# Sums of halves of the normalised input on GpSimd or VectorE, ahead of three seven-product stages

## The chip, the cores and the metric

One core of a Trainium2 chip runs the whole program. The time is the device time of one execution in microseconds (us). The engines named are TensorE (PE in the profile), VectorE (DVE), ScalarE (ACT), GpSimd (POOL), and SyncE (SP), which issues most of the loads of weights.

## The reference

Two blocks of a network on a sequence of 512 positions of 1024 features, in float32. The first block puts 16 learned positions in front (528 in all) and has two layers. Each layer is a mixer, a layer norm, a multilayer perceptron with squared ReLU, and a layer norm:

```python
h = _layer_norm(DEEPNORM_ALPHA * h + mix, ln_g[layer, 0], ln_b[layer, 0])
h = _layer_norm(DEEPNORM_ALPHA * h + _sq_relu_mlp(h, ffn_w1[layer], ffn_w2[layer]),
                ln_g[layer, 1], ln_b[layer, 1])
```

with `_sq_relu_mlp(h, w1, w2) = square(relu(h @ w1)) @ w2`. The mixer of layer 0 is an attention, that of layer 1 a retention, which begins with `proj = h @ w_in`. The second block (sparse attention beside a state-space scan, then a gated feed-forward part) comes behind them. The change touches only the first matrix product behind three of the layer norms: the perceptron's `h @ w1` of layer 0 (behind the norm ln00) and of layer 1 (behind ln10), and the retention's `h @ w_in` (behind ln01).

## The kernel before, in words

**Layout and arithmetic.** The activations lie in `x32`, features on the 128 partitions: 8 tiles (KT) of 528 columns, a column for each position. Every matrix product is made of three fast ones: each operand is split into a high part and a rest (`x_hi`, `x_lo`; `w_hi`, `w_lo`), and TensorE adds hi x hi, hi x lo and lo x hi. ScalarE makes the high parts (`split_hi`, L362, for weights), VectorE the rests (`split_lo`, L370). Weights come in chunks of 128 x 1024 into a ring of four (`raw`), and each engine's program splits three chunks ahead (AHEAD) of the chunk that TensorE multiplies.

**The norm and the first tiles.** At the end of a layer norm VectorE scales tile after tile (L1404), ScalarE writes the normalised tile to `x32` (L1434, counted by the semaphore `norm_y`) and its high part to `x_hi` (L1437), and VectorE the rest to `x_lo` (L1410, counted by `norm_lo`). TensorE starts while this goes on: `first_two` multiplies two chunks at the same time, tile by tile, and before each of the eight tiles it waits for that tile's `x_lo`. The last tile is number 7.

**Seven products.** A product of a 2 x 2 grid of blocks is made of seven block products instead of eight, for which sums of halves of both operands are needed. Sums of halves of the weights are made in memory by DMAs that GpSimd issues (`SUM_PARTS`, L327 to L349). Sums of halves of the input are made by `turn_sum` (L1461 to L1471), four of them, each of 128 x 1056 elements (128 x 1024 in layer 1's perceptron): 

```python
(t1, x[:, 0:4, first], x[:, 0:4, second], ALU.subtract),
(t2, t1, x[:, 4:8, second], ALU.add),
(self.fourth(), t2, x[:, 4:8, first], ALU.subtract),
(t3, x[:, 4:8, second], x[:, 0:4, second], ALU.subtract)
```

Sum 1 waits for all eight tiles (`norm_y`), sums 2 and 3 for the one before each (`turns_made`). `turn_hi` (ScalarE, L1477) and `turn_lo` (VectorE, L1486 and L1488) split them, number 0 to 3 in the order in which TensorE reads them. TensorE's `seven_pe` (L1546) waits for `turns_lo` at the first block of the kinds 5, 6, 7 and 4.

**Order of the work around the change.** Each engine has one queue in program order, written out by hand. Behind ln00 and ln10 stands the stage "up" (`up0a`, `up1a`): four chunks in the ordinary way, two of them in `first_two`. Behind it comes `seven0a` or `seven1a`. `Mlp.act` and `Mlp.dve` say what ScalarE and VectorE do during "up": ScalarE evicts each tile (`positive`, L1702), VectorE squares it (`square`, L1742), ScalarE takes the high part (`high`, L1706), VectorE the rest (`low`, L1746), with `split(0)` to `split(3)` and the turns between. Each `positive(t)` for t of 2 or more waits for `square(t - 2)`, since the buffers are two. `last_parts` puts turn_lo of 2 and 3 into the first blocks of the seven-product stage. Behind ln01 stands `ret0`, four chunks, then `sevenr0`; `retention_act` and `retention_dve` give the order there.

In the seven-product stage ScalarE copies block products out of PSUM (L1609) and VectorE adds the next ones to the copies (L1647); TensorE waits for a copy before it goes on in the same bank.

**GpSimd's queue** is `even_loads`, `ret_loads`, `dsa_loads`. `ret_loads` issues the copies and sums of the weights of later stages, each behind a wait for a chunk that TensorE has done, and the load of `decay` for each retention head, the first of them behind the last `x_lo` of ln01 (L1824). GpSimd does no arithmetic in the first block but a few memsets. In the second block it adds `select` and `bias_near` (L2307), 64 times, beside VectorE's work of the sparse attention.

Of the kernel before, what the change touches and what calls it, by code (L numbers as in the profile page):

```python
# [7 lines left out]
ALU = mybir.AluOpType  # L8
# [6 lines left out]
KT = D // P  # L15
# [187 lines left out]
def program(nc, x_in, weights, params, tables, lam_in, w_uk, w_uv, rel, line, skewed, cum_dram, acum_dram, merged_dram, kept_dram, gate_dram, sums_dram, out):  # L203
    with ExitStack() as ctx:
# [10 lines left out]
        x32 = sb("x32", [P, KT, T])  # L215
# [257 lines left out]
        for p, (kind, h, j) in enumerate(products):  # L473
            n = sum(len(m) for m in maps.values())
# [676 lines left out]
        def only_split(eng, split, name):  # L1151
# [8 lines left out]
        norm_squared, norm_var, norm_root, norm_scaled, norm_y, norm_hi, norm_lo = (  # L1160
            sem(f"norm_{n}") for n in ("squared", "var", "root", "scaled", "y", "hi", "lo"))
        mlp_squared, hidden_hi, hidden_lo = sem("mlp_squared"), sem("hidden_hi"), sem("hidden_lo")
        seven_done, seven_summed, seven_kept = (sem(f"seven_{n}") for n in ("done", "summed", "kept"))
        turns_made, turns_hi, turns_lo = (sem(f"turns_{n}") for n in ("made", "hi", "lo"))
# [274 lines left out]
        class Halves:  # L1439
# [13 lines left out]

                return self.fourth_rows.rearrange("p a (k n) -> p (a k) n", k=2)[:, :, 0:self.w]

            def source(self, dve, norm):

                dve.wait_ge(norm_y, KT * (norm.nl + 1))
                return x32

            def turn_sum(self, dve, norm, n):  # L1461
                first, second, w = self.cols(0), self.cols(1), self.w
# [92 lines left out]
        class Mlp(Halves):  # L1555
# [138 lines left out]
            def act(self, act, next_norm):  # L1694
                name = f"up{self.layer}a"

                def positive(t):
                    u = FIRST_TILE[name] + t
                    act.wait_ge(chunk_done, FIRST_CHUNK[name] + t + 1)
                    wait(act, mlp_squared, 32 * self.layer + t - 1)  # L1700
                    src = early_out(t, self.wide) if t < 2 else tile_out(Step(u), self.wide)
                    nc.scalar.activation(halves(self.pos[:, t % 2], self.wide), src, ACT.Relu).then_inc(evicted[u % 2], 1)  # L1702

                def high(t):
                    act.wait_ge(mlp_squared, 32 * self.layer + t + 1)
                    nc.scalar.activation(halves(self.h_hi[:, t], self.wide), halves(self.sq[:, t % 2], self.wide), ACT.Copy).then_inc(hidden_hi, 1)  # L1706

                def split(t):
                    split_hi(act, Step(FIRST_CHUNK[name] + t + AHEAD))
                split(0)  # L1710
                self.turn_hi(act, 0)
                self.turn_hi(act, 1)
                positive(0)
                positive(1)
                split(1)
                high(0)
                high(1)
                positive(2)
                split(2)
                self.turn_hi(act, 2)  # L1720
                positive(3)
                high(2)
                split(3)
                high(3)
                self.turn_hi(act, 3)
                for half, hn in enumerate("ab"):
                    self.seven_act(act, f"seven{self.layer}{hn}")
                    if half:
                        before_norm_act(act, f"down{self.layer}{hn}", next_norm)
                    else:  # L1730
                        only_split(act, split_hi, f"down{self.layer}{hn}")

            def dve(self, dve, norm, next_norm):
                name = f"up{self.layer}a"

                def square(t):
                    u = FIRST_TILE[name] + t
                    dve.wait_ge(evicted[u % 2], u // 2 + 1)
                    if t >= 2:
                        dve.wait_ge(hidden_lo, 32 * self.layer + t - 1)  # L1740
                    pos, sq = halves(self.pos[:, t % 2], self.wide), halves(self.sq[:, t % 2], self.wide)
                    nc.vector.tensor_tensor(sq, pos, pos, ALU.mult).then_inc(mlp_squared, 1)  # L1742

                def low(t):
                    dve.wait_ge(hidden_hi, 32 * self.layer + t + 1)
                    nc.vector.tensor_tensor(halves(self.h_lo[:, t], self.wide), halves(self.sq[:, t % 2], self.wide),  # L1746
                                            halves(self.h_hi[:, t], self.wide), ALU.subtract).then_inc(hidden_lo, 1)

                def split(t):
                    split_lo(dve, Step(FIRST_CHUNK[name] + t + AHEAD))  # L1750
                self.turn_sum(dve, norm, 0)
                self.turn_sum(dve, norm, 1)
                split(0)
                self.turn_lo(dve, 0)
                square(0)
                square(1)
                split(1)
                low(0)
                low(1)
                self.turn_sum(dve, norm, 2)  # L1760
                self.turn_sum(dve, norm, 3)
                square(2)
                self.turn_lo(dve, 1)
                split(2)
                square(3)
                low(2)
                split(3)

                def last_parts():
                    self.turn_lo(dve, 2)  # L1770
                    low(3)
                    self.turn_lo(dve, 3)
                for half, hn in enumerate("ab"):
                    self.seven_dve(dve, f"seven{self.layer}{hn}", None if half else last_parts)
                    if half:
                        before_norm_dve(dve, f"down{self.layer}{hn}", 1.0, next_norm)
                    else:
                        residual_dve(dve, f"down{self.layer}{hn}", self.wide, ALPHA)

        ln00 = LayerNorm("ln00", FIRST_TILE["up0a"], True, PARAM["ln_g"], PARAM["ln_b"])  # L1780
        mlp0 = Mlp(0, True)
# [28 lines left out]
        def ret_loads(pool):  # L1810

            for part in SUM_PARTS:
                part(pool, 2)
            for h, name in ((2, "down0a"), (3, "down0b")):
                pool.wait_ge(chunk_done, FIRST_CHUNK[name])
                for part in SUM_PARTS:
                    part(pool, 1 + h)
            for h in range(RET_HEADS):
                if h == 0:
                    pool.wait_ge(norm_lo, ln01.lo_at)  # L1820
                else:
                    pool.wait_ge(ret_decayed, 5 * h)
                a = TABLE["decay"] + h * DECAYS
                pool.dma_start(decay[:], tables[:, a:a + DECAYS]).then_inc(decay_in, 16)  # L1824
                pool.wait_ge(chunk_done, FIRST_CHUNK[("sevenr1", "ro0", "ro1", "ret_out1")[h]])
                for part in ((sums_copy,), (sums_of_two,), (sums_of_three, sums_of_four), ())[h]:
                    part(pool, 5)
            for name, parts in (("ret_out1", SUM_PARTS[:2]), ("down1a", SUM_PARTS[2:])):
                pool.wait_ge(chunk_done, FIRST_CHUNK[name])
                for part in parts:  # L1830
                    part(pool, 6)
            pool.wait_ge(chunk_done, FIRST_CHUNK["down1b"])
            for part in SUM_PARTS:
                part(pool, FFN_SUMS)
            sums_copy(pool, FFN_SUMS + 1)

        class Retention(Halves):
# [14 lines left out]
            def part(self, h, i, row, half):  # L1852

                kind, n = self.pairs(h)[i]
                skip = META if kind in "qg" and half == 0 else 0
                start = half * HALF - (META if kind in "qg" and half else 0)
                buf = {"q": rq, "k": rk, "v": v_raw, "g": rg}[kind]
                return buf[:, 2 * n + row, start:start + HALF - skip], slice(skip, HALF)
# [78 lines left out]
        ret = Retention()  # L1937
# [238 lines left out]

        def retention_dve(dve):
            for c in range(4):
                if c < 2:
                    ret.turn_sum(dve, ln01, 2 * c)  # L2180
                    ret.turn_sum(dve, ln01, 2 * c + 1)
                split_lo(dve, Step(FIRST_CHUNK["ret0"] + c + AHEAD))
                if c < 3:
                    ret.turn_lo(dve, c)
            ret.turn_lo(dve, 3)
            for h in range(RET_HEADS):
                ret.dve(dve, h)
                if h in (1, 2):
                    for ck in range(4):
                        split_lo(dve, Step(FIRST_CHUNK[f"ro{h - 1}"] + ck + AHEAD))  # L2190
                        ret_residual_dve(dve, h - 1, ck, ALPHA if h == 1 else 1.0)
                ret_keys_dve(dve, h)
            split_lo(dve, Step(FIRST_CHUNK["ret_out1"] + AHEAD))
            for n in range(8):
                ret_gate_dve(dve, LAST_HEAD, n)
            for e in range(4):
                ret_lo_dve(dve, LAST_HEAD, e)
            before_norm_dve(dve, "ret_out1", 1.0, ln10, outs=[open_out(t) for t in range(OPEN)], split_before=1)
# [1578 lines left out]
```

## Time and profile before

| | us |
|---|---|
| median of 3 runs | 2663.25 |
| lowest and highest | 2659.4, 2663.29 |
| span of the profiled execution, first to last instruction | 2656.4 |
| TensorE busy | 2615.0 (98%) |
| VectorE busy | 1675.5 (63%) |
| ScalarE busy | 1268.0 (48%) |
| GpSimd busy | 183.4 (7%) |

The profile is of one execution; what lies around its span (3.0 to 6.9 us against the three runs) isn't in the trace, and its own time is not given beside the page. Starts are in us from the start of the span. A row of a timeline has the start, the length, the engine, the line of the kernel, the operation, what it writes and reads, the shape, how many instructions are merged in the row, and in brackets how long the engine stood idle before it and who released it. In the chain that ended last TensorE has 85% of the span, VectorE 8%, ScalarE 4%. TensorE's granted clock was 1.00 in all stretches around the change.

### The profile page before, as it was taken

Reading aid. Unit: us, or ns where it says so; the run is one execution under the profiler, and the core shown is the slowest. Engines: PE = TensorE matmul, PEld = TensorE weight load, DVE = VectorE, ACT = ScalarE, POOL = GpSimd, SP = SyncE. Lnnn points to the kernel's source line nnn. Section 1 sums busy time; section 2 is a strip of 40 time slices with the busy share of each in tenths; the row PEclk is TensorE's granted clock in tenths of the full one; section 3 lists DMA queues with packets and bytes.
Section 4 is the critical chain, followed back from the end, with each engine's and each line's share of the span. In section 5 each row is a group of like instructions: output and inputs, shape, how many; then the busy total and the mean of one; then the engine's idle time right before and its main releaser. Section 6 shows DMA issues by size and latency. Waiting matters only on the chain.

```text
span 2656.4 us, 42476 instructions
## 1 busy us (share of the span) xinstructions
PE 2615.0 (98%) x16497; PEld 2236.1 (84%) x16497; DVE 1675.5 (63%) x2902; ACT 1268.0 (48%) x2049; POOL 183.4 (7%) x234
## 2 busy tenths in 40 slices
PE   9999999999999999999999999999999999999998
PEld 9877799999999798779898786766877777799996
DVE  4544586264565465487265535875589987696784
ACT  4556365153454354365154434254365564475561
POOL 1111000000000000100000012051000000000000
PEclk9999999999999999999999999999999999999999
DMA  9994936858556564736557979922433333254451
GB/s 355 222 230 119 216 92 234 207 165 248 135 171 212 146 184 140 232 110 196 145 164 245 260 187 266 253 66 80 145 94 114 119 111 120 81 189 148 156 174 56
DMA packets 187722, 450.56 MB, mean 170 GB/s; under 512 B 14984, under 2 KB 31368, under 8 KB 186896
## 3 DMA queue, kind: packets, MB, share of 16 engines
q1 hardware_dynamic: 108368, 264.29, 29.4%
q0 software_dynamic: 60000, 167.78, 26.7%
q10 hardware_dynamic: 19168, 15.93, 2.0%
q8 instruction: 127, 2.08, 0.3%
q14 instruction: 59, 0.48, 0.1%
HBM read 438.24 MB, written 159.51 MB: 225 GB/s over the span
## 4 chain that ended last, share of the span: by engine, by line
PE 85%; DVE 8%; ACT 4%; issue 2%; DMA 0%; POOL 0%; DVEq 0%; ACTq 0%; POOLq 0%
PE ps L399 29%; PE ps L1546 25%; PE ps L549 6%; PE ps L3344 4%; PE ps L2354 2%; PE ps L1991 2%; PE ps L2145 2%; PE ps L2029 2%; PE ps L2891 2%; PE ps L791 2%; PE ps L919 2%; DVE w_lo L370 1%; PE ps L878 1%; ACT w_hi L362 1%; DVE xs L3044 1%
## 5 line engine op out<-in xcount | busy, mean ns | idle before, releaser
L370 DVE TENSOR_TENSOR w_lo<-raw,w_hi 128x1024 fp32r<-128x1024 f32 x500 | 611.1, 1223 | 467.1 <-ACT w_hi L362 466.1
L362 ACT ACTIVATE w_hi<-raw 128x1024 fp32r<-128x1024 f32 x500 | 527.1, 1055 | 512.9 <-PE ps L399 292.3
L1546 PE MATMUL ps<-x_hi,w_hi 128*128 128x264 f32 (+1 forms) x1120 | 317.4, 283 | 2.1 <-DVE rg L1925 0.7
L1546 PE MATMUL ps<-x_hi,w_lo 128*128 128x264 f32 (+1 forms) x1120 | 316.3, 282 | 0.0
L1546 PE MATMUL ps<-x_lo,w_hi 128*128 128x264 f32 (+1 forms) x1120 | 316.1, 282 | 0.0
L399 PE MATMUL ps<-x_hi,w_hi 128*128 128x512 f32 (+1 forms) x688 | 248.3, 378 | 4.4 <-DVE x_lo L1410 2.7
L399 PE MATMUL ps<-x_lo,w_hi 128*128 128x512 f32 (+1 forms) x688 | 244.3, 372 | 0.0
L399 PE MATMUL ps<-x_hi,w_lo 128*128 128x512 f32 (+1 forms) x688 | 243.2, 371 | 0.0
L1546 PEld LDWEIGHTS ps<-x_hi,w_hi 128*128 128x128 f32 x1120 | 210.8, 188 | 5.0 <-issue 2.2
L1546 PEld LDWEIGHTS ps<-x_hi,w_lo 128*128 128x128 f32 x1120 | 211.1, 188 | 0.0
L1546 PEld LDWEIGHTS ps<-x_lo,w_hi 128*128 128x128 f32 x1120 | 210.6, 188 | 0.4
L399 PE MATMUL ps<-h_hi,w_hi 128*128 128x264 f32 (+1 forms) x768 | 205.7, 322 | 0.0
L399 PE MATMUL ps<-h_lo,w_hi 128*128 128x264 f32 (+1 forms) x768 | 205.1, 322 | 0.0
L399 PE MATMUL ps<-h_hi,w_lo 128*128 128x264 f32 (+1 forms) x768 | 204.6, 320 | 0.0
L399 PEld LDWEIGHTS ps<-x_hi,w_hi 128*128 128x128 f32 x688 | 124.6, 188 | 39.3 <-issue 16.4
L399 PEld LDWEIGHTS ps<-x_hi,w_lo 128*128 128x128 f32 x688 | 124.6, 188 | 23.3
L399 PEld LDWEIGHTS ps<-x_lo,w_hi 128*128 128x128 f32 x688 | 124.5, 188 | 22.8 <-issue 1.0
L399 PEld LDWEIGHTS ps<-h_lo,w_hi 128*128 128x128 f32 x768 | 127.7, 188 | 11.6 <-issue 0.2
L399 PEld LDWEIGHTS ps<-h_hi,w_lo 128*128 128x128 f32 x768 | 127.8, 189 | 11.2
L399 PEld LDWEIGHTS ps<-h_hi,w_hi 128*128 128x128 f32 x768 | 127.1, 188 | 11.6 <-issue 0.2
L549 PE MATMUL ps<-x_hi,w_hi 128*128 128x264 f32 x352 | 111.9, 318 | 0.0
L549 PE MATMUL ps<-x_lo,w_hi 128*128 128x264 f32 x352 | 99.9, 284 | 0.0
(503 smaller groups left out, 5827.8 us busy)
## 6 DMA issues: line engine op xcount, KB each, us to landing
raw<-in_weights SPq DMA_DIRECT2D x255, 512.0 KB
raw<-weight_sums SPq DMA_DIRECT2D x280, 256.0 KB
weight_sums<-in_weights POOLq DMA_DIRECT2D x36, 1536.0 KB, 19.4
raw<-in_weights SPq DMA_DIRECT2D x210, 256.0 KB
weight_sums<-in_weights POOLq DMA_DIRECT2D x12, 2048.0 KB, 31.1
weight_sums<-in_weights POOLq DMA_DIRECT2D x12, 1792.0 KB, 22.1
weight_sums<-weight_sums POOLq DMA_DIRECT2D x12, 1536.0 KB, 14.3
weight_sums<-weight_sums POOLq DMA_DIRECT2D x4, 2048.0 KB, 19.7
```

Source lines behind the costliest of these rows:

```text
L362: nc.scalar.activation(w_hi[:, s], raw[:, s], ACT.Copy).then_inc(hi_ready, 1)
L370: nc.vector.tensor_tensor(w_lo[:, s], raw[:, s], w_hi[:, s], ALU.subtract).then_inc(lo_ready, 1)
L399: last = nc.tensor.matmul(o[:, h, :], w[:, s, k], a[:, k0 + k, cols], start=start and k == 0 and n == 0, stop=stop and k == nk - 1 and n == 2)
L549: last = nc.tensor.matmul(ps[:, 2 + h, 0:HALF], a[:, g % RING, w], b[:, k, cols], start=k == 0 and n == 0, stop=half_end and n == 2)
L791: last = nc.tensor.matmul(flat[0:n, o + a:o + b], qk[rows, qt, c:c + n], qk[rows, kt_, a:b], start=True, stop=True)
L919: last = nc.tensor.matmul(flat[rows, 3072 + (first - 1) * P:3072 + SEQ], vt[0:k, group_of(p) % 2, b, col:col + wide], turned_from(p, b, fi ...
L1546: last = nc.tensor.matmul(out_, w[:, s, 4 * (b % 2) + k], a, start=kind in "125" and k == n == 0, stop=k == 3 and n == 2, skip_group_check ...
L1991: last = nc.tensor.matmul(flat[:, o + SEQ - w:o + SEQ], rv[0:n, b, e * P:(e + 1) * P], decayed[0:n, b, SEQ - w:SEQ], start=b == 0, stop=b ...
L2029: last = nc.tensor.matmul(ps[:, 2 * (u % 2), 0:SEQ], w[:, g % RING, 2 * f + m], a[:, f], start=f == 0 and n == 0, stop=f == 3 and n == 2)
L2145: last = nc.tensor.matmul(open_out(t)[:, 0, :], w[:, g % RING, k], a[:, k % 4], start=k == 0 and n == 0, stop=k == KT - 1 and n == 2)
L2354: last = nc.tensor.matmul(kept_out_at(n)[:, 0, :], w[:, ck % RING, k], a[:, k, META:T], start=k == 0 and i == 0, stop=k == KT - 1 and i == 2)
L3344: last = nc.tensor.matmul(out_, w[:, g % RING, n], a[:, r], start=n == 0 and m == 0, stop=n == len(rows) - 1 and m == 2)
```

## The change

`turn_sum_pool` does with GpSimd what `turn_sum` does with VectorE, and is called for the three stages from `ret_loads`. The twelve calls of `turn_sum` go from VectorE's queue. On ScalarE `positive(0)` moves ahead of `turn_hi(1)`, and on VectorE `square(0)` ahead of `turn_lo(0)`. The stage ahead of `sevenf` in the second block keeps `turn_sum` on VectorE.

```diff
+            def turn_sum_pool(self, pool, norm, n):
+                first, second, w = self.cols(0), self.cols(1), self.w
+                t1, t2, t3 = (self.t_raw[:, m, :, 0:w] for m in range(3))
+                if n == 0:
+                    pool.wait_ge(norm_y, KT * (norm.nl + 1))
+                if n in (1, 2):
+                    pool.wait_ge(turns_made, 4 * self.turn + n)
+                out_, a, b, op = ((t1, x32[:, 0:4, first], x32[:, 0:4, second], ALU.subtract),
+                                  (t2, t1, x32[:, 4:8, second], ALU.add),
+                                  (self.fourth(), t2, x32[:, 4:8, first], ALU.subtract),
+                                  (t3, x32[:, 4:8, second], x32[:, 0:4, second], ALU.subtract))[n]
+                nc.gpsimd.tensor_tensor(out_, a, b, op).then_inc(turns_made, 1)
...
                 split(0)
                 self.turn_hi(act, 0)
+                positive(0)
                 self.turn_hi(act, 1)
-                positive(0)
                 positive(1)
...
-                self.turn_sum(dve, norm, 0)
-                self.turn_sum(dve, norm, 1)
                 split(0)
+                square(0)
                 self.turn_lo(dve, 0)
-                square(0)
                 square(1)
                 split(1)
                 low(0)
                 low(1)
-                self.turn_sum(dve, norm, 2)
-                self.turn_sum(dve, norm, 3)
                 square(2)
...
             for part in SUM_PARTS:
                 part(pool, 2)
+            for n in range(4):
+                mlp0.turn_sum_pool(pool, ln00, n)
             for h, name in ((2, "down0a"), (3, "down0b")):
...
                 if h == 0:
+                    for n in range(4):
+                        ret.turn_sum_pool(pool, ln01, n)
                     pool.wait_ge(norm_lo, ln01.lo_at)
...
                     part(pool, 6)
+                if name == "ret_out1":
+                    for n in range(4):
+                        mlp1.turn_sum_pool(pool, ln10, n)
             pool.wait_ge(chunk_done, FIRST_CHUNK["down1b"])
...
         def retention_dve(dve):
             for c in range(4):
-                if c < 2:
-                    ret.turn_sum(dve, ln01, 2 * c)
-                    ret.turn_sum(dve, ln01, 2 * c + 1)
                 split_lo(dve, Step(FIRST_CHUNK["ret0"] + c + AHEAD))
```

## Rows read from the trace of the kernel before

**Rows 1.** The page: its first line, and busy time, share and count of TensorE.

```profile
span 2656.4 us, 42476 instructions
...
PE 2615.0 (98%) x16497; PEld 2236.1 (84%) x16497; DVE 1675.5 (63%) x2902; ACT 1268.0 (48%) x2049; POOL 183.4 (7%) x234
```

**Rows 2.** Timeline of TensorE in seven0a and seven1a (start, length, instruction, [idle before]).

```profile
385.25 0.39 PE L1546 MATMUL ps<-t_hi,w_hi 128*128 128x264 f32 x1 [0.55 <-ACT h_u L1609]
...
394.55 0.40 PE L1546 MATMUL ps<-x_hi,w_hi 128*128 128x264 f32 x1 [0.25 <-DVE h_z L1647]
...
1195.48 0.39 PE L1546 MATMUL ps<-t_hi,w_hi 128*128 128x256 f32 x1 [0.58 <-ACT h_u L1609]
...
1204.66 0.38 PE L1546 MATMUL ps<-x_hi,w_hi 128*128 128x256 f32 x1 [0.39 <-DVE h_z L1647]
```

**Rows 3.** GpSimd's groups by form (busy, mean ns), and one addition in its timeline.

```profile
L2307 POOL TENSOR_TENSOR combo<-select,bias_near 128x256 f32<-128x256 f32 x48 | 35.2, 757 | 31.1 <-DVE d_stat L2585 31.1
...
L2307 POOL TENSOR_TENSOR combo<-select,bias_near 128x128 f32<-128x128 f32 x16 | 7.0, 459 | 6.1 <-DVE d_stat L2585 6.0
...
1732.84 0.72 POOL L2307 TENSOR_TENSOR combo<-select,bias_near 128x256 f32<-128x256 f32 x1
```

**Rows 4.** Timelines of VectorE and GpSimd where an addition met VectorE's work.

```profile
1730.38 1.22 DVE L370 TENSOR_TENSOR w_lo<-raw,w_hi 128x1024 fp32r<-128x1024 f32 x1 [1.51 <-ACT w_hi L362]
...
1730.48 1.71 POOL L2307 TENSOR_TENSOR combo<-select,bias_near 128x256 f32<-128x256 f32 x1
...
1738.10 2.26 DVE L2601 TENSOR_SCALAR d_buf<-d_buf,d_stat 128x384 f32<-128x384 f32 x1
...
1739.42 0.71 POOL L2307 TENSOR_TENSOR combo<-select,bias_near 128x256 f32<-128x256 f32 x1
...
1740.28 0.41 DVE L2601 TENSOR_SCALAR d_buf<-d_buf,d_stat 128x384 f32<-128x384 f32 x1
```

**Rows 5.** Timelines of ScalarE, VectorE and TensorE from ln00 into the stage up0a.

```profile
364.48 0.83 ACT L1434 ACTIVATE x<-ln_xc,par 128x528 f32<-128x528 f32 x1
...
366.02 0.71 DVE L1410 TENSOR_TENSOR x_lo<-x,x_hi 128x528 fp32r<-128x528 f32 x1 [0.79 <-ACT x_hi L1437]
...
366.65 1.25 DVE L1471 TENSOR_TENSOR t_raw<-x 128x1056 f32<-128x1056 f32 x1
...
367.00 0.40 PE L399 MATMUL ps<-x_hi,w_hi 128*128 128x264 f32 x2
...
369.55 1.22 DVE L370 TENSOR_TENSOR w_lo<-raw,w_hi 128x1024 fp32r<-128x1024 f32 x1
...
381.02 0.71 DVE L1742 TENSOR_TENSOR h_sq<-h_pos 128x528 f32<-128x528 f32 x1 [0.21 <-ACT h_pos L1702]
...
382.37 0.63 ACT L1706 ACTIVATE h_hi<-h_sq 128x528 fp32r<-128x528 f32 x1
```

**Rows 6.** The same from ln01 into ret0 and the first block of sevenr0.

```profile
732.27 0.83 ACT L1434 ACTIVATE x<-ln_xc,par 128x528 f32<-128x528 f32 x1
...
734.67 0.47 PE L399 MATMUL ps<-x_hi,w_hi 128*128 128x512 f32 x1
...
747.86 0.29 PE L1546 MATMUL ps<-x_hi,w_hi 128*128 128x264 f32 x1
```

**Rows 7.** Timeline of ScalarE from ln10 into the stage up1a.

```profile
1175.54 0.82 ACT L1434 ACTIVATE x<-ln_xc,par 128x512 f32<-128x512 f32 x1
...
1192.64 0.62 ACT L1706 ACTIVATE h_hi<-h_sq 128x512 fp32r<-128x512 f32 x1
```

**Rows 8.** Timelines of GpSimd around the three places, and of VectorE at decay's first reader.

```profile
443.47 1.68 POOL L327 DMA_DIRECT2D weight_sums<-in_weights  x2 [118.57 <-PE ps L1546]
...
734.82 0.60 POOL L1824 DMA_DIRECT2D decay<-in_tables  x1 [45.90 <-DVE x_lo L1410]
...
791.07 0.69 DVE L2077 SCALAR_TENSOR_TENSOR decayed<-ps,decay 128x512 f32<-128x512 f32 x1 [1.36 <-PE ps L1968]
...
1252.46 1.50 POOL L344 DMA_DIRECT2D weight_sums<-weight_sums  x1 [134.29 <-PE ps L1546]
```

More of the change, by code:

```diff
@@ L1454, in fourth @@
                 return self.fourth_rows.rearrange("p a (k n) -> p (a k) n", k=2)[:, :, 0:self.w]
-            def source(self, dve, norm):
-                dve.wait_ge(norm_y, KT * (norm.nl + 1))
-                return x32
+            def turn_sum_pool(self, pool, norm, n):
[10 more added lines that the diff above has]
+                nc.gpsimd.tensor_tensor(out_, a, b, op).then_inc(turns_made, 1)
             def turn_sum(self, dve, norm, n):
```

## Prediction, on record before the changed kernel had run

> **What bounds the kernel now.** I read the page first. TensorE is busy 98% of the span [rows 1], so a part that moves off VectorE pays only where TensorE stands still for VectorE. The next view is TensorE's timeline from the end of each of the three layer norms (the last tile of the normalised input is there at 365.3, 733.1 and 1176.4 us) to the first dozen blocks of the seven-product stage. In stage seven0a there are two pauses, 0.55 us behind ScalarE's copy L1609 and 0.25 us behind VectorE's sum L1647; in seven1a the same two, 0.58 and 0.39 us; in the retention stage there is none [rows 2]. The reader should see that all the idle time in reach is 0.55 + 0.25 + 0.58 + 0.39 = 1.77 us, 0.07% of the span. Such a change can't be a clear gain; the question is what it can cost.
>
> **What is removed.** Twelve VectorE instructions, four a stage, of 1.25 us in the record. From one start to the next it is 0.08 us less (the last x_lo has 0.71 us, and the sum behind it starts 0.63 us later), so 1.17 us each and 4.7 us a stage [rows 5]. Two stand ahead of the first weight split, right behind the last x_lo, two in the middle of the stage "up". What hid them is TensorE's work on the four tiles of "up" (or of ret0), and that cover stays.
>
> **What is added: twelve GpSimd instructions.** The trace before has no GpSimd addition of this size. The nearest rows are L2307's: 757 ns for 256 columns and 459 ns for 128 in the mean, 0.72 us for one of 256 that nothing disturbed [rows 3]. The slope is (757 - 459)/128 = 2.33 ns a column. From the mean, 1056 columns take 0.757 + 800 x 0.00233 = 2.62 us. The mean holds some disturbed ones; with the undisturbed 0.72 less the 0.459 of 128 the slope is 2.04 ns, and the time 0.72 + 800 x 0.00204 = 2.35 us. I take 2.5 us, between two near ends; four make 10 us, twice what VectorE took. Alone they would do no harm: in the first stage sum 1 would be ready at 367.9, sum 2 near 370.7 and the last by 376.
>
> **Whether the two engines can work at the same time** decides. Near 1730 us VectorE began a weight split w_lo (two inputs in SBUF) 0.10 us ahead of a GpSimd addition. The split took its usual 1.22 us; the addition took 1.71 us instead of 0.72, so it waited for the whole of the split [rows 4]. The other order is there for another VectorE form: a TENSOR_SCALAR that met additions under way took 2.26 us against 0.41 us for its twin just after, so it got free at 1738.10 + 2.26 - 0.41 = 1739.95, 0.2 us before the last record of the GpSimd run ended at 1740.13 [rows 4]. No row shows a two-input VectorE instruction meeting an addition in the middle. Its cost lies between nothing (it goes on, as that w_lo did over the last 0.13 us of the GpSimd record before it) and the rest of the addition, 2.5 - 0.2 = 2.3 us. I take 2.3 us: the split and the addition shut each other out in the one case where they met, and the reverse is seen with a VectorE instruction that asks for less data. Its own ends are 2.35 - 0.2 = 2.15 us and the full 2.62 us.
>
> The Trainium skill (SBUF — State Buffer, section "Who interferes with whom") says that a VectorE instruction with two SBUF inputs contends with a GpSimd instruction that reads SBUF, and that the second to issue is blocked until the first is done. By it the sum below stands; if it held for no two-input instruction the sum would be about -0.6 us. The trace agrees for one order, with the 1.71 us; the other is not shown for this form.
>
> **Stage seven0a, step by step.** GpSimd waits for norm_y. ScalarE's last tile ends at 364.48 + 0.83 = 365.31, so sum 1 starts at about 365.4. The last x_lo (L1410) is issued at 366.02, since it waits for one more ScalarE instruction [rows 5]. So sum 1 is always first, by 0.6 us. In the old order the sums were queued behind this x_lo; now it stands behind a sum. It goes at 365.4 + 2.3 = 367.7 and ends at 368.4 instead of 366.73. TensorE's last column of the first two tiles began at 367.00 [rows 5] and needs it; with 0.15 us from release to start it begins at 368.55: 1.55 us lost at once.
>
> Then both queues are full. The three other sums and VectorE's work take turns, and VectorE has no idle time in which to hide them. Up to square(3) it has three w_lo (1.22 - 0.08 = 1.14 us from start to start), two turn_lo (of the sums' size, 1.17), four squares and two h_lo (of x_lo's size, 0.62) [rows 5]: 3.4 + 2.3 + 3.7 = 9.5 us rounded. Starting 0.6 us after 367.7, square(3) is done at 368.3 + 9.5 + 3 x 2.3 = 384.7. Before it ended at 381.73, and h_hi of that tile started at 382.37, because ScalarE's own queue was not there sooner [rows 5]. Now h_hi waits for VectorE and starts at 384.8, 2.4 us late. Behind it on ScalarE stand turn_hi(3), a w_hi and the copy L1609 for which TensorE was already waiting at 385.25 [rows 2]. So that block comes at 387.7: 2.4 us in all for the stage, the 1.55 included, not beside it.
>
> **Stage seven1a**: the last tile ends at 1176.36 [rows 7], sums of 1024 columns take 0.1 us less, so x_lo gets free at 1178.65; 0.6 + 9.3 + 3 x 2.2 = 16.5 us later, 1195.15, square(3) is done, and h_hi starts at 1195.2 instead of 1192.64 [rows 7]: 2.6 us.
>
> **Retention stage**: x_lo goes at 733.10 + 0.1 + 2.3 = 735.5, TensorE at 736.35 instead of 734.67 [rows 6]: 1.7 us. There are no squares and no h_lo here. VectorE reaches the w_lo that the first of the seven products needs after x_lo, one w_lo, a turn_lo and the three later sums, at about 736.1 + 1.1 + 1.2 + 3 x 2.3 = 745.3, so it is done at 746.5; TensorE asked for it at 747.86 before and asks at 749.6 now [rows 6]. Nothing more is lost.
>
> **Edits at nothing.** GpSimd's queue: it stood idle for 118.6 us before 443.47 and for 134.3 us before 1252.46, so nothing is late behind the sums of the first and third stage; behind those of the second is the load of decay, moved from 734.82 to near 745. Its first reader is at 791.07 [rows 8], which leaves 45 us. No other queue is passed. positive(0) ahead of turn_hi(1) on ScalarE costs nothing while square(0) is hidden; turn_hi(1) comes a microsecond later, and positive(1) with it, ahead of squares that VectorE reaches later still. The third user, the stage before sevenf, keeps its sums on VectorE.
>
> **The sum** is 2.4 + 1.7 + 2.6 = 6.7 us. With 2.15 us for each hold it is 5.4 (four holds on the path in two stages, one in the third), with 2.62 us 9.6. The profiled execution has a span of 2656.4 us [rows 1]; the three runs lie 3.0 to 6.9 us above it, for what stands around the span and for scatter. Its own time isn't given, so I add the sum to the median: 2663.25 + 6.7 = 2670.0 us.
>
> **Rivals.**
> - No hold in the order that matters: VectorE's two-input work goes on beside GpSimd. For it speaks that w_lo over the end of a GpSimd record; against it the addition that waited 1.0 us. VectorE then is free 4.7 us earlier and the pauses that it ends itself, 0.25 + 0.39 = 0.64 us, go; ScalarE's copies after TensorE's own work keep theirs. 2662.6 us, 2661.5 if all four went: not slower. It decides if the last x_lo keeps its 0.7 us in all stages.
> - Held only once a stage: after x_lo VectorE's queue keeps GpSimd out until VectorE waits for a sum itself, in time that it has gained. 1.55 + 1.7 + about 1.55 = 4.8 us, 2668.0 us. For it speaks that VectorE was first in the one clean meeting.
> - The additions run much slower than the slope says (rows of 264 with a stride, three reads in each stage from x): at twice 2.5 us each hold is 2.5 us longer, four on the path in two stages and one in the third, 6.7 + 9 x 2.5 = 29 us, 2692 us. Nothing in the trace asks for it.
>
> **How the numbers follow.** Forecast 0.60, no hold 0.26, held once 0.09, far slower sums 0.05. A measurement of this kernel can tell about 0.2%, 5.3 us, from no change. The forecast's own range is 5.4 to 9.6 us, and with the scatter of the runs (3.9 us among three) a fifth of it may still fall inside 5.3: slower 0.60 x 0.82 + 0.05 + 0.02 = 0.56; same 0.11 + 0.22 + 0.07 = 0.40; faster 0.04, from the rival without holds and a low set of runs. The range of 8 in 10 goes from 2661.0, which takes in most of that rival, to 2675.0, above the forecast's upper end of 2672.9 with scatter; alone, the forecast's range is 2667.5 to 2674.
>
> **What would show it.** Right: in each stage the last x_lo in the record lasts about 2.4 us, or starts that late, and TensorE pauses 1.5 us before the eighth column of "up"; the first GpSimd sum takes 2.5 us, the next ones more; VectorE's w_lo and turn_lo there show 2 to 3.5 us; the wait of seven0a behind L1609 grows from 0.55 to some 1.4 us. Wrong: x_lo at 0.7 us with a GpSimd sum running beside it, or TensorE's gaps at the same places and lengths as before.

## The result, and the profile after

The changed kernel takes 2666.82 us (median of 20 runs, 2664.39 to 2673.91) against 2659.36 us (20 runs beside it, 2658.09 to 2664.36): ratio 1.0026, 95% interval 1.0019 to 1.0032. That is 6.9 us slower by the ratio (5.1 to 8.5) and 7.5 us by the two medians, where 6.7 was forecast. In absolute terms the forecast of 2670.0 is 3.2 us high, because it stood on a median of three runs (2663.25) that was itself 3.9 us above that of the twenty.

The page of the changed kernel, the lines that answer to [rows 1]:

```profile
span 2663.2 us, 42470 instructions
...
PE 2615.6 (98%) x16497; PEld 2236.1 (84%) x16497; DVE 1685.9 (63%) x2890; ACT 1268.2 (48%) x2049; POOL 218.3 (8%) x246
```

The span is 6.8 us longer, TensorE's busy time is the same within 0.6 us: TensorE waits more. VectorE is busy 10.4 us more with twelve instructions fewer, so others of its instructions last longer. GpSimd's four sums of the first stage, in its timeline:

```profile
365.50 2.45 POOL L1467 TENSOR_TENSOR t_raw<-x 128x1056 f32<-128x1056 f32 x1 [36.65 <-ACT x L1434]
...
368.04 2.81 POOL L1467 TENSOR_TENSOR t_raw<-t_raw,x 128x1056 f32<-128x1056 f32 x1
...
370.93 3.34 POOL L1467 TENSOR_TENSOR h_raw<-t_raw,x 128x1056 f32<-128x1056 f32 x1
...
374.21 2.94 POOL L1467 TENSOR_TENSOR t_raw<-x 128x1056 f32<-128x1056 f32 x1
```

The first took 2.45 us, from the moment when the tile was there; the others 2.81 to 3.34 us. The excess is time in which VectorE's instruction was still at work: x_lo ended at 368.52, 0.48 us behind the start of sum 2, and 2.81 less 0.48 is 2.33. The next view is the timeline of VectorE, and its last row that of ScalarE, in the same stretch; they answer to [rows 5]:

```profile
366.13 2.39 DVE L1410 TENSOR_TENSOR x_lo<-x,x_hi 128x528 fp32r<-128x528 f32 x1 [0.80 <-ACT x_hi L1437]
...
368.44 3.48 DVE L370 TENSOR_TENSOR w_lo<-raw,w_hi 128x1024 fp32r<-128x1024 f32 x1
...
371.86 2.98 DVE L1750 TENSOR_TENSOR h_sq<-h_pos 128x528 f32<-128x528 f32 x1
...
374.76 3.52 DVE L1496 TENSOR_TENSOR t_lo<-t_raw,t_hi 128x1056 fp32r<-128x1056 f32 x1
...
384.12 0.69 DVE L1750 TENSOR_TENSOR h_sq<-h_pos 128x528 f32<-128x528 f32 x1
...
384.84 0.65 ACT L1714 ACTIVATE h_hi<-h_sq 128x528 fp32r<-128x528 f32 x1 [0.62 <-DVE h_sq L1750]
```

Each of the first four VectorE rows has its usual length plus a hold: x_lo 2.39 us instead of 0.71, w_lo 3.48 instead of 1.22, a square 2.98 instead of 0.70, turn_lo 3.52 instead of 1.25. The two queues take turns: if each hold ends one usual length before its row does, x_lo got free at 367.81, 0.14 us before sum 1's record ended, then sum 2 when x_lo was done, w_lo when sum 2 nearly was, and so on. Four VectorE rows a stage are held in this way, and the twelve holds, less the twelve sums that VectorE no longer makes, are its 10.4 us. Square(3) ended at 384.81 instead of 381.73, and h_hi waited for it. All pauses of TensorE in the three stages, which answer to [rows 2], [rows 6] and [rows 7]:

```profile
368.67 0.36 PE L399 MATMUL ps<-x_hi,w_hi 128*128 128x264 f32 x1 [1.40 <-DVE x_lo L1410]
...
387.74 0.39 PE L1554 MATMUL ps<-t_hi,w_hi 128*128 128x264 f32 x1 [1.28 <-ACT h_u L1617]
...
397.04 0.39 PE L1554 MATMUL ps<-x_hi,w_hi 128*128 128x264 f32 x1 [0.28 <-DVE h_z L1655]
...
738.81 0.47 PE L399 MATMUL ps<-x_hi,w_hi 128*128 128x512 f32 x1 [1.55 <-DVE x_lo L1410]
...
1183.72 0.47 PE L399 MATMUL ps<-x_hi,w_hi 128*128 128x512 f32 x1 [1.44 <-DVE x_lo L1410]
...
1202.40 0.39 PE L1554 MATMUL ps<-t_hi,w_hi 128*128 128x256 f32 x1 [1.67 <-ACT h_u L1617]
...
1211.58 0.39 PE L1554 MATMUL ps<-x_hi,w_hi 128*128 128x256 f32 x1 [0.43 <-DVE h_z L1655]
```

Ahead of the eighth column of "up" (and of ret0) it now waits 1.40, 1.55 and 1.44 us, where it had waited for nothing. Behind L1609 (now L1617) the pauses grew from 0.55 and 0.58 to 1.28 and 1.67 us. The second pauses, 0.28 and 0.43 us, are within 0.04 us of what they were.

To see where the span grew I take the starts of the last x_lo but one of each norm, which stand ahead of every sum, as marks. The three stretches begin at the marks of ln00, ln01 and ln10, and the last one ends with the span. Each holds one of the three stages, so a difference is what that stage cost:

| kernel | marks (us) | stretches (us) | more than before |
|---|---|---|---|
| before | 364.52, 732.31, 1175.59 | 367.79, 443.28, 1480.8 | |
| changed | 364.63, 734.76, 1179.79 | 370.13, 445.02, 1483.4 | 2.34, 1.74, 2.6 |

The forecast was 2.4, 1.7 and 2.6.

### The profile page after: what moved, and what is told of

Its sections match the earlier page's. It is cut to its first block, busy times and chain, and to the rows that moved or that the text cites. A ratio compares the mean times of both kernels' runs of the same rounds, so it can differ in the third digit from the quotient of the medians.

```text
span 2663.2 us, 42470 instructions
## 1 busy us (share of the span) xinstructions
PE 2615.6 (98%) x16497; PEld 2236.1 (84%) x16497; DVE 1685.9 (63%) x2890; ACT 1268.2 (48%) x2049; POOL 218.3 (8%) x246
## 4 chain that ended last, share of the span: by engine, by line
PE 83%; DVE 10%; ACT 4%; issue 2%; DMA 0%; POOL 0%; DVEq 0%; ACTq 0%; POOLq 0%
PE ps L399 27%; PE ps L1554 25%; PE ps L549 6%; PE ps L3352 4%; PE ps L2362 2%; PE ps L2002 2%; PE ps L2156 2%; PE ps L2040 2%; DVE w_lo L370 2%; PE ps L2899 2%; PE ps L791 2%; PE ps L919 2%; PE ps L878 1%; ACT w_hi L362 1%; DVE xs L3052 1%
## 5 line engine op out<-in xcount | busy, mean ns | idle before, releaser
L370 DVE TENSOR_TENSOR w_lo<-raw,w_hi 128x1024 fp32r<-128x1024 f32 x500 | 619.9, 1240 | 466.2 <-ACT w_hi L362 465.2
L549 PE MATMUL ps<-x_hi,w_lo 128*128 128x264 f32 x352 | 99.9, 284 | 0.0
```

The lines of the kernel that those rows point to most:

```text
L370: nc.vector.tensor_tensor(w_lo[:, s], raw[:, s], w_hi[:, s], ALU.subtract).then_inc(lo_ready, 1)
L549: last = nc.tensor.matmul(ps[:, 2 + h, 0:HALF], a[:, g % RING, w], b[:, k, cols], start=k == 0 and n == 0, stop=half_end and n == 2)
```

## The experiments

**My theory:** a GpSimd addition and a VectorE instruction with two inputs in SBUF shut each other out, in turns, and that lengthens VectorE's rows. **The rivals:** that the loss comes from the new order or from sums ready too late; that any GpSimd work on SBUF does it; that a run of GpSimd instructions keeps VectorE out until it ends. All experiments were timed against the kernel before on the same chip.

**Order alone.** All sums on VectorE, only the two moves.

```diff
                 self.turn_hi(act, 0)
+                positive(0)
                 self.turn_hi(act, 1)
-                positive(0)
...
                 split(0)
+                square(0)
                 self.turn_lo(dve, 0)
-                square(0)
```

> The two moves of order alone (positive(0) ahead of turn_hi(1), square(0) ahead of turn_lo(0)), all sums on VectorE as before. Theory (GpSimd's additions and VectorE's two-input work shut each other out): nothing of the loss is here, the time is that of the kernel before within 1 us, and no VectorE instruction lasts longer. Rival (the new order delays ScalarE's chain): some 1 to 3 us slower, with the pauses of 0.55 and 0.58 us behind L1609 grown.

Measured: ratio 1.0000 (0.9991 to 1.0009), stretches 367.80, 443.30, 1480.6. TensorE's first pause in seven0a, in its timeline:

```profile
385.19 0.39 PE L1546 MATMUL ps<-t_hi,w_hi 128*128 128x264 f32 x1 [0.55 <-ACT h_u L1609]
```

It is the pause of before. The order carries none of the loss.

**One stage alone.** Only the retention stage's sums on GpSimd.

```diff
+                    for n in range(4):
+                        ret.turn_sum_pool(pool, ln01, n)
                     pool.wait_ge(norm_lo, ln01.lo_at)
...
-                if c < 2:
-                    ret.turn_sum(dve, ln01, 2 * c)
-                    ret.turn_sum(dve, ln01, 2 * c + 1)
```

> Only the retention stage's four sums go to GpSimd, the perceptrons keep theirs on VectorE. Theory: 1.7 us slower than before, all of it as one pause of TensorE ahead of the eighth column of ret0, while the last x_lo lasts 2.4 us. Rival (the loss is that sums are ready late and turn_hi and turn_lo wait for them): no loss here, since TensorE reads the first turned half more than 10 us after sum 1, and x_lo lasts 0.7 us.

Measured: ratio 1.0009 (1.0000 to 1.0018). The stretches of the perceptrons are 367.75 and 1480.8, as before, the middle one 445.02: 1.74 us, all of it in the stage that was changed. TensorE's timeline:

```profile
736.21 0.48 PE L399 MATMUL ps<-x_hi,w_hi 128*128 128x512 f32 x1 [1.55 <-DVE x_lo L1410]
```

The pause alone is 1.55 us, more than ten microseconds before TensorE reads a turned half, and it ends with x_lo, which needs no sum. Late sums can't be its cause.

**Sums after x_lo.** GpSimd's first sum waits for the last x_lo.

```diff
                 if n == 0:
-                    pool.wait_ge(norm_y, KT * (norm.nl + 1))
+                    pool.wait_ge(norm_lo, norm.lo_at)
```

> As changed, but GpSimd's first sum of each stage waits for the last x_lo (norm_lo) instead of the last normalised tile. Theory (both queues take turns, so what counts is the sum of both): the pauses of 1.4 to 1.6 us ahead of the eighth column go in all three stages, and the retention stage costs nothing; in the two perceptrons a fourth hold moves behind x_lo, square(3) ends at about 366.65 + 9.5 + 4 x 2.3 = 385.35 us, and the block behind L1609 comes 3.0 us later than before. In all about 6 us slower than before less what the second pause gives back (0.6), so 5 to 6 us. Rival (only the hold of x_lo costs): at most 1 us slower than before.

Measured: ratio 1.0036 (1.0023 to 1.0050), 9.6 us above before where I had said 5 to 6. The interval overlaps the changed kernel's (1.0019 to 1.0032), so the times alone don't order the two. The stretches do: they are 3.2, 2.1 and 3.5 us longer than before, 8.9 us in all, where the changed kernel's were 6.7. x_lo lasted 0.71 us at most, and no pause stood ahead of the eighth column. TensorE's timeline behind it:

```profile
383.91 0.39 PE L1554 MATMUL ps<-x_hi,w_hi 128*128 128x264 f32 x1 [0.43 <-DVE w_lo L370]
...
388.07 0.39 PE L1554 MATMUL ps<-t_hi,w_hi 128*128 128x264 f32 x1 [0.97 <-DVE w_lo L370]
...
391.56 0.39 PE L1554 MATMUL ps<-t_hi,w_hi 128*128 128x264 f32 x1 [1.77 <-ACT h_u L1617]
...
755.61 0.36 PE L1554 MATMUL ps<-x_hi,w_hi 128*128 128x264 f32 x1 [1.21 <-ACT rq L2173]
...
760.61 0.39 PE L1554 MATMUL ps<-t_hir,w_hi 128*128 128x264 f32 x1 [0.39 <-ACT r_u L1894]
```

ScalarE's timeline ahead of the pause at 755.61:

```profile
753.90 1.08 ACT L1485 ACTIVATE t_hir<-t_rawr 128x1056 fp32r<-128x1056 f32 x1 [4.53 <-POOL t_rawr L1467]
...
754.89 0.58 ACT L2173 ACTIVATE rq<-ps 128x512 f32<-128x512 f32 x1
```

The rival (only x_lo's hold costs) is out: that hold is gone, and the loss is not the 1 us at most that it allowed. In the perceptrons the block behind L1609 came 3.2 and 3.5 us later against the marks, near the 3.0 that I had worked out, and the second pauses gave nothing back. The main miss is in the retention stage, where I had seen no reader in time: there ScalarE's turn_hi, which waited for the last sum, stands ahead of the eviction `rq`. So later sums delay the eviction that TensorE needs before it enters sevenr0 (1.21 us), and a copy after it (0.39 us).

**First sum twice.** An extra addition into a place that is written again later.

```diff
+                if n == 0:
+                    nc.gpsimd.tensor_tensor(t3, a, b, op)
                 nc.gpsimd.tensor_tensor(out_, a, b, op).then_inc(turns_made, 1)
```

> As changed, with the first sum of each stage made twice, the extra one first, into a place that is written again later; same waits. Theory of turns: VectorE's x_lo is held by one addition only, so TensorE's pause ahead of the eighth column stays 1.4 to 1.6 us in all three stages; the extra 2.3 us end up before square(3), so each perceptron loses 2.3 us more and the retention stage nothing: 4.6 us above the changed kernel, 11.5 us above before. Rival (a run of GpSimd instructions keeps VectorE out until the run ends): x_lo lasts 4.8 us, the pause is 4 us in each stage, and the retention stage too loses 2.4 us more: 7 us above the changed kernel.

Measured: ratio 1.0052 (1.0038 to 1.0066), 13.8 us above before; stretches 4.6, 3.7 and 4.8 us longer. The first GpSimd row, two of VectorE and two of TensorE from the timelines:

```profile
365.43 2.45 POOL L1468 TENSOR_TENSOR t_raw<-x 128x1056 f32<-128x1056 f32 x1 [37.78 <-ACT x L1434]
...
366.06 2.39 DVE L1410 TENSOR_TENSOR x_lo<-x,x_hi 128x528 fp32r<-128x528 f32 x1 [0.80 <-ACT x_hi L1437]
...
368.37 3.47 DVE L370 TENSOR_TENSOR w_lo<-raw,w_hi 128x1024 fp32r<-128x1024 f32 x1
...
368.59 0.36 PE L399 MATMUL ps<-x_hi,w_hi 128*128 128x264 f32 x1 [1.40 <-DVE x_lo L1410]
...
755.41 0.36 PE L1556 MATMUL ps<-x_hi,w_hi 128*128 128x264 f32 x1 [1.02 <-ACT rq L2175]
```

x_lo lasted 2.39 us, as in the changed kernel, and the pauses ahead of the eighth column stayed at 1.40, 1.56 and 1.43 us although the next addition was already queued. So a two-input VectorE instruction is let in between two additions: turns, not runs. In the perceptrons the extra 2.3 us came as expected. The retention stage lost 1.9 us more than in the changed kernel, where I had said nothing, through the same eviction as above (1.02 us).

**Memsets for sums.** The sums of halves are left out; GpSimd only writes.

```diff
-                nc.gpsimd.tensor_tensor(out_, a, b, op).then_inc(turns_made, 1)
+                out_ = (self.t_raw[:, 0:3, :, 0:w], self.t_raw[:, 1:3, :, 0:w], out_, out_)[n]
+                nc.gpsimd.memset(out_, 0.0).then_inc(turns_made, 1)
```

> As changed, but each of GpSimd's twelve sums is a memset of the same place (the first of a stage of 3 x 1056 columns, to last some 2.5 us, the second of 2 x 1056, the others of 1056): the sums of halves are left out, and GpSimd reads nothing from SBUF, while all waits, the order and the places written stay. Theory (what shuts out is reading: both engines fetch operands from SBUF): the last x_lo lasts 0.7 us, TensorE does not pause ahead of the eighth column, every VectorE row has its usual length, and the time is that of before or up to 1 us less, since VectorE has twelve instructions fewer. Rival 1 (any GpSimd work on SBUF holds VectorE): x_lo lasts 2 us or more and most of the 6.9 us stays. Rival 2 (the loss comes from the order and from the sums' waits): the loss stays as far as the memsets take as long as the sums.

Measured: ratio 1.0000 (0.9991 to 1.0009), stretches 367.79, 443.30, 1480.7. GpSimd's first memset, VectorE beside it, and TensorE's first pause:

```profile
365.25 2.76 POOL L1468 MEMSET t_raw<- 128x3168 f32 x1 [39.13 <-ACT x L1434]
...
365.91 0.71 DVE L1410 TENSOR_TENSOR x_lo<-x,x_hi 128x528 fp32r<-128x528 f32 x1 [0.79 <-ACT x_hi L1437]
...
366.86 1.23 DVE L370 TENSOR_TENSOR w_lo<-raw,w_hi 128x1024 fp32r<-128x1024 f32 x1 [0.24 <-ACT w_hi L362]
...
385.16 0.39 PE L1555 MATMUL ps<-t_hi,w_hi 128*128 128x264 f32 x1 [0.53 <-ACT h_u L1618]
```

The memset ran for 2.76 us, over the whole of x_lo and nearly all of w_lo, and neither grew. The waits, the order and, all four taken together, the places written are those of the changed kernel, and the first memset of a stage lasts longer than its sum did (the later ones are shorter), but nothing is read: every VectorE row of the stage has its usual length, and the whole loss is gone. With the copy below this settles the cause. It also shows what freeing VectorE of twelve sums is worth: nothing in the trace. All four pauses of before are still there, 0.53, 0.27, 0.58 and 0.39 us.

**Copies for sums.** One input; the first of a stage has 3 x 1056 columns. The sums of halves are left out.

```diff
-                nc.gpsimd.tensor_tensor(out_, a, b, op).then_inc(turns_made, 1)
+                if n == 0:
+                    out_ = self.t_raw[:, :, :, :].rearrange("p m k n -> p (m k) n")
+                    b = x32[:, 0:6, :].rearrange("p k (h n) -> p (k h) n", h=2)
+                nc.gpsimd.tensor_copy(out_, b).then_inc(turns_made, 1)
```

> As changed, but each sum is a GpSimd copy with one input (the first of a stage of 3 x 1056 columns, to last some 2.9 us, the others of 1056 columns, about 1.1 us each): the sums of halves are left out. Theory: one read stream is enough to shut VectorE's two-input work out, so x_lo waits for the copy to end (about 2.2 us, or 2.7 with its own work) and TensorE pauses 1.8 us ahead of the eighth column in each stage; the later copies are short, so the two perceptrons lose no more than that and the total is 4 to 6 us above before. Rival (only GpSimd's two-input form collides): x_lo lasts 0.7 us and the time is that of before.

Measured: ratio 1.0044 (1.0030 to 1.0058), 11.7 us, twice what I had said; each stretch is 3.5 or 3.6 us longer. GpSimd's copy, x_lo, and a pair of TensorE's products right behind and well behind the pause:

```profile
365.40 2.84 POOL L1470 COPY t_raw<-x 128x3168 f32<-128x3168 f32 x1 [36.89 <-ACT x L1434]
...
366.05 2.75 DVE L1410 TENSOR_TENSOR x_lo<-x,x_hi 128x528 fp32r<-128x528 f32 x1 [0.79 <-ACT x_hi L1437]
...
368.94 0.63 PE L399 MATMUL ps<-x_hi,w_hi 128*128 128x264 f32 x2 [1.76 <-DVE x_lo L1410]
...
374.19 0.41 PE L399 MATMUL ps<-x_hi,w_hi 128*128 128x264 f32 x2
```

An instruction with one input is enough: x_lo waited almost for the copy's end. But the pause is 1.76 us and the stage lost 3.5. The rest is in TensorE's own rows, 0.63 us for a pair of products that takes 0.41 us at full clock. The windows have the reason (stretch, length, then busy time and count of PE, PEld, DVE, ACT and POOL, then the granted clock, the share of DMA and GB/s). First three of this kernel, then one of the changed kernel behind its pause of 1.40 us:

```profile
369.00:371.00 2.00, 2.00 (x10) 2.00 (x11) 1.80 (x1) 0.86 (x3) 1.94 (x2) 0.53 0.04 8
...
371.00:373.00 2.00, 2.00 (x13) 2.00 (x13) 1.87 (x2) 2.00 (x4) 2.00 (x2) 0.62 0.45 96
...
373.00:375.00 2.00, 2.00 (x19) 2.00 (x18) 2.00 (x3) 1.07 (x3) 0.22 (x1) 1.00 0.46 166
```

```profile
369.00:371.00 2.00, 2.00 (x19) 2.00 (x18) 2.00 (x1) 0.81 (x3) 1.92 (x2) 1.00 0.04 8
```

The clock stood near half, which is the lower of its levels of 1.2 and 2.4 GHz, for about 3.5 us behind the pause, and that costs the other 1.7 us. In the other two stages, behind pauses of 1.89 and 1.86 us, it fell as far, but only when TensorE had been busy again for about 1.0 and 1.3 us. In the changed kernel it stayed at 1.00.

**A shorter copy.** The first copy has 2 x 1056 columns; the sums of halves are left out again.

```diff
-                    out_ = self.t_raw[:, :, :, :].rearrange("p m k n -> p (m k) n")
-                    b = x32[:, 0:6, :].rearrange("p k (h n) -> p (k h) n", h=2)
+                    out_ = self.t_raw[:, 0:2, :, :].rearrange("p m k n -> p (m k) n")
+                    b = x32[:, 0:4, :].rearrange("p k (h n) -> p (k h) n", h=2)
```

> As the kernel with GpSimd copies in place of the sums, but the first copy of a stage has 2 x 1056 columns instead of 3 x 1056, so about 1.9 us instead of 2.8 us; the sums of halves are left out. The longer copy cost 3.5 us a stage where TensorE's pause was 1.8 to 1.9 us; in the rows TensorE's granted clock stood at half for some 3.5 us behind that pause and at full behind the changed kernel's pauses of 1.4 to 1.55 us. Theory (shut-out sets the pause, and the rest of that kernel's loss is the clock's fall behind the pause): x_lo now lasts about 1.8 us, the pause is 0.9 us, the clock stays at full, and the stages cost 0.9 us each, some 3 us in all above before. Rival (each copy costs something besides the pause, whatever the clock): about 2.6 us a stage, 8 us in all.

Measured: ratio 1.0010 (1.0002 to 1.0019), 2.7 us where I had said 3; stretches 1.1, 1.2 and 1.2 us longer, behind pauses of 0.89, 1.04 and 1.00 us. The same rows, and the window behind the pause:

```profile
367.00 1.95 POOL L1470 COPY t_raw<-x 128x2112 f32<-128x2112 f32 x1 [39.09 <-ACT x L1434]
...
367.64 1.87 DVE L1410 TENSOR_TENSOR x_lo<-x,x_hi 128x528 fp32r<-128x528 f32 x1 [0.80 <-ACT x_hi L1437]
...
369.65 0.36 PE L399 MATMUL ps<-x_hi,w_hi 128*128 128x264 f32 x1 [0.89 <-DVE x_lo L1410]
```

```profile
371.00:373.00 2.00, 2.00 (x18) 2.00 (x18) 2.00 (x3) 2.00 (x4) 2.00 (x2) 1.00 0.13 40
```

A copy 0.9 us shorter made the pause 0.9 us shorter and the stage 2.3 to 2.4 us cheaper, and the clock stayed at 1.00. The rival (2.6 us a stage whatever the clock) is out. So the long copy's loss is its hold plus the clock.

**Two changes of order on the kernel before.** TensorE's four pauses there, 1.77 us in all, come from ScalarE's queue (two) and from an unbroken row of VectorE work (two). ScalarE idled ahead of `positive(3)`, and VectorE ahead of the seven products.

```diff
                 self.turn_hi(act, 2)
-                positive(3)
                 high(2)
                 split(3)
+                positive(3)
                 high(3)
...
                 low(2)
                 split(3)
+                self.turn_lo(dve, 2)
...
-                    self.turn_lo(dve, 2)
                     low(3)
                     self.turn_lo(dve, 3)
```

With ScalarE's move alone:

> The kernel before, all sums on VectorE, with high(2) and split(3) ahead of positive(3) on ScalarE, into the 1.4 us in which it waited for TensorE's fourth tile. If the pauses of 0.55 and 0.58 us behind L1609 come from ScalarE's queue alone, as its rows say, both go and VectorE's need not change: 1.1 us faster, ratio 0.9996. If they come from VectorE, nothing moves.

Measured: ratio 0.9998 (0.9989 to 1.0007), which can't be told from no change. In the trace both pauses behind L1609 are gone and the first and the last stretch are 0.5 and 0.7 us shorter, 1.2 us in all where 1.1 was forecast, which is too little for these runs to show in the time. With both moves:

> The same, and turn_lo(2) on VectorE ahead of the seven-product stage, where VectorE stood idle for 1.2 us, instead of in its first blocks. If the second pauses (0.25 and 0.39 us ahead of L1546, released by the sum L1647) come from VectorE's unbroken row of instructions there, all four pauses go: 1.8 us faster than before, ratio 0.9993. Otherwise as the kernel with ScalarE's order alone.

> The kernel with both changes of order and all sums on VectorE, timed once more, since its first interval (0.9987 to 1.0005) takes in no change while its profile has the four pauses gone and the stretches of the two perceptrons 1.1 us shorter each. If those stretches tell the time: ratio 0.9992, within 0.0003. If the first medians were chance: 1.0000.

Measured: ratio 0.9996 (0.9987 to 1.0005) the first time, 0.9986 (0.9978 to 0.9995) the second: by the ratios 1 to 4 us faster. The second interval excludes no change, the first does not; the forecasts, 0.9993 and 0.9992, lie in both. In the first trace the stretches are 1.1, 0 and 1.1 us shorter; in the second the first and the last are 1.2 and 0.9 us shorter and the middle one is 0.1 us longer. The windows of seven0a and seven1a in the first trace (length, busy time of TensorE first):

```profile
366.00:402.00 36.00, 36.00 (x296) 35.85 (x295) 32.19 (x40) 24.52 (x35) 0.00 (x0) 1.00 0.50 149
...
1177.00:1215.00 38.00, 37.93 (x269) 35.41 (x268) 34.44 (x43) 25.97 (x39) 0.00 (x0) 1.00 0.53 162
```

TensorE is busy for all of the first 36.00 us and for 37.93 of the other 38.00. Both intervals lie wholly below the changed kernel's, so this version is faster than that; that it is faster than the kernel before rests on the second interval and on the two traces. It keeps the sums on VectorE.

## Why the prediction was right, step by step

- **The bound.** "Such a change can't be a clear gain" held: with VectorE relieved and nothing held, the memset kernel had the time of before.
- **Length of a sum.** 2.5 us taken from L2307's slope, 2.45 us measured where nothing held it.
- **The hold.** 2.3 us from the start of the sum taken; in the record x_lo has 2.39 us where it had 0.71, so it was held for 1.68 us, and it started 0.63 us behind the sum: 2.31 us. The three holds behind it are 2.26 to 2.28 us. The reverse order, which no row of before had shown for a two-input instruction, was the open step, and it is now shown: memset and copy tell that GpSimd's reading is what holds. Before, only the other order had been seen for this form, so to take 2.3 us and not nothing was a choice, which the forecast gave 0.60, and not a reading.
- **Stage seven0a.** Against the mark, 0.11 us later than before: TensorE at 368.56 (368.55 forecast), square(3) done at 384.70 (384.7), h_hi at 384.73 (384.8), the block behind L1609 at 387.63 (387.7). The 1.55 us ahead of the eighth column are included in the stage's 2.4, as forecast: sparing them brought nothing when the sums came after x_lo.
- **Retention stage and seven1a.** 1.7 and 2.6 us forecast, 1.74 and 2.6 measured. In the retention stage the w_lo that TensorE needs first was done at 748.95, or 746.5 when the 2.45 us by which the mark is later are taken off, as worked out. GpSimd's load of decay moved to 747.81 and cost nothing.
- **"Nothing more is lost" in the retention stage** was right for this change but on thin ground: I had checked VectorE's w_lo and not ScalarE's eviction behind turn_hi. With the last sum done 2.1 us later against the mark (sums after x_lo) or 3.6 us later (first sum twice) TensorE waited for that eviction for 1.2 and 1.0 us.
- **Rivals.** No hold: out, x_lo lasted 2.39, 2.40 and 2.32 us in the three stages. The gain that I gave it, 0.64 us from the pauses behind L1647, was wrong too: in the memset kernel, where nothing was held, they stayed at 0.27 and 0.39 us. They went only when turn_lo(2) was moved. Held once a stage: out, four VectorE rows in a stage are held. Much slower sums: out, 2.45 us.
- **The level.** 3.2 us high, from a median of three runs.

What stays open: why a VectorE TENSOR_SCALAR was kept out over more than one addition [rows 4], while the two-input instructions took turns; no run tried it.

## What to carry to other kernels

Before work moves to GpSimd, ask what it reads and what VectorE does at the same time: where VectorE's queue was full of two-input work, each GpSimd addition of 2.45 us kept VectorE out until 2.2 to 2.3 us after its start, twice the 1.17 us that it had taken as VectorE's own. GpSimd work that only writes took nothing. And look at which queue each pause of the bounding engine comes from: here two small moves within ScalarE's and VectorE's order removed the pauses that relieving VectorE left as they were.

## What the runs showed that I had not expected

- A GpSimd memset of 2.76 us beside VectorE's two-input work held nothing, while a copy of 2.84 us held x_lo almost to its end. The Trainium skill (SBUF — State Buffer, section "Who interferes with whom") says that a VectorE instruction with two SBUF inputs contends with a GpSimd instruction that reads SBUF and not with one that only writes it. These rows agree on both counts.
- TensorE's granted clock fell to about half (0.53, and 0.50 from 741.2 to 744.0 us) behind pauses of 1.76 to 1.89 us ahead of the eighth column, and not behind pauses of 1.40 to 1.56 us at the same place. Nor did it fall behind pauses of 1.77 us later on, behind L1609, in the kernels with sums after x_lo and with the first sum twice (1.00 in the 2 us after the one in seven0a). So the length of one pause alone does not decide it; what does was not tried. Where it fell, the stage lost 3.5 us or a little more for a pause of 1.76 to 1.89 us, about twice its length.
